# A float32 encoder trunk: two of the last projection's four column groups computed as seven products of half blocks

## The chip, the cores and the metric

The kernel runs on one core of a Trainium2 chip. Its engines are TensorE (PE; a weight load is PEld), VectorE (DVE), ScalarE (ACT), GpSimd (POOL) and SyncE (SP), which issues most of the transfers. They run side by side, each through its own list of instructions in order, and meet only in semaphores: an instruction waits until a counter has a value, and raises another when it is done. The metric is the device time of one launch in microseconds; lower is better.

## The reference

```python
for i in range(DEPTH):                       # DEPTH = 2: attention mixer, then conv mixer
    xn = _rmsnorm(x, norm_gain[i])
    y = _diff_attention(xn, ...) if i % 2 == 0 else _conformer_conv(xn, ...)
    x = x + y
return _rmsnorm(x, final_gain)

def _conformer_conv(xn, w_in, b_in, dw, dw_b, ln_g, ln_b, w_out, b_out):
    a, g, z = jnp.split(xn @ w_in + b_in, [CONV_WIDTH, 2 * CONV_WIDTH], axis=-1)
    u = a * jax.nn.sigmoid(g)
    u = depthwise_conv(u, dw) + dw_b         # 31 taps along the sequence
    u = silu(layernorm(u) * ln_g + ln_b)
    return (u * jax.nn.silu(z)) @ w_out + b_out
```

Shapes: x is 256 x 2048, every matrix float32. What changes is the last matrix product, `(u * silu(z)) @ w_out`, 256 x 2048 by 2048 x 2048, with the bias, the residual sum and the final norm around it.

## The kernel before, in words

**Products.** Each float32 product is made of three passes over operands that TensorE reads quickly: every operand is split into a high part (a rounded copy, by ScalarE, L476 for weights) and a low part (what is left, one subtraction of the operand and its high part: by VectorE at L826, by GpSimd at L448), and high x high, high x low and low x high are added up in PSUM.

**Weights.** They come in chunks of 128 x 4 x 512 (1 MB) through a ring of four raw buffers. SyncE loads chunk c when the low part of chunk c - 4 is made (`low_part_ready`, L317); ScalarE makes the high part, then VectorE or GpSimd the low part. `by_pool` (L298) says which: in most of the conv's input projection and the first four chunks of its output projection GpSimd, afterwards VectorE.

**Output projection of the conv.** Its 2048 columns are four groups of 512, each four chunks long (16 tiles of 128 along the contraction). For each tile there are two row tiles of x and three passes: 96 matmuls of 512 columns a group (`project`, L1237). The left operand is conv_hi and conv_lo. Before it lie the layer norm and the gating: VectorE normalises (L1118), ScalarE applies silu into PSUM banks (L673), VectorE multiplies with zT in place in PSUM (L1127, `gate_block`), ScalarE makes the high part (L681) and VectorE the low part (L1131, `block_lo`), eight blocks of two tiles each, which the first group waits for two by two. The counter s_lo counts them.

**Around it.** The bias and the final gain, each 128 x 2048, are loaded when s_lo is complete (L410, L412). VectorE adds the bias to the residual stream xs (L1163) and the product of each group to it (L1171), ScalarE sums squares (L785), VectorE multiplies by the gain (L1177). The last group is computed row tile by row tile on a bank that holds the bias and the residual already.

**Earlier stages that matter here.** After the attention's output projection VectorE turns x1 (L1017), makes its low parts (L1025), and works through low parts, the scaling of the first input group (L1070) and then 480 taps of the depthwise conv (L1065), in that order. Behind the taps come column sums, statistics, and a broadcast of them by TensorE (L1403), which TensorE reaches in its own order.

## Time and profile before

| | us |
|---|---|
| median of 3 runs (lowest, highest) | 827.04 (825.95, 827.09) |
| the profiled execution | 826.85 |
| its span, first to last instruction | 825.1 |
| TensorE busy | 817.6 |
| VectorE busy | 645.7 |
| ScalarE busy | 450.1 |
| GpSimd busy | 228.8 |

The mean granted clock of TensorE is 0.999 of full speed. "Busy" counts the time in which an instruction of the engine ran; in a timeline, "x4" at a row's end is the number of instructions merged into it, and what stands in brackets is the idle time before and what ended it.

### The profile page before, as it was taken

What the parts mean: (1) busy time and instruction counts of PE and PEld (TensorE: products, weight loads), DVE (VectorE), ACT (ScalarE), POOL (GpSimd) and SP (SyncE); (2) the same over time, 40 slices, a digit from 0 to 9 for tenths busy, and PEclk for the clock granted to TensorE, in tenths of its full rate; (3) what the DMA queues carried; (4) which work ended last, traced back from release to release, by engine and by line L of the source; (5) the groups of instructions that cost most, each with busy time, mean ns of one, the idle gap of its engine ahead of it and who ended that gap; (6) DMA issues with size and microseconds to landing.
All of it is one profiled execution on the core that took longest, in us unless ns stands there. A gap on an engine that the chain in (4) does not pass through costs nothing.

```text
span 825.1 us, 13852 instructions
## 1 busy us (share of the span) xinstructions
PE 817.6 (99%) x5628; PEld 756.1 (92%) x5628; DVE 645.7 (78%) x1099; ACT 450.1 (55%) x590; POOL 228.8 (28%) x107
## 2 busy tenths in 40 slices
PE   9999999999999999999999999999999999999996
PEld 9998899889998899888888999999999999998885
DVE  7578785697659785798788988999999998656651
ACT  7756643546436643556544465465555556694432
POOL 0300000000000000002000009988989887680000
PEclk9999999999999999999999999999999999999999
DMA  9987566536654566525655666655655565549502
GB/s 330 394 290 272 173 204 216 192 122 205 227 187 146 171 212 212 189 102 173 228 175 189 204 193 215 204 175 185 204 191 175 197 203 176 185 154 355 195 10 102
DMA packets 99809, 163.68 MB, mean 198 GB/s; under 512 B 3616, under 2 KB 40992, under 8 KB 99240
## 3 DMA queue, kind: packets, MB, share of 16 engines
q1 hardware_dynamic: 98128, 160.51, 57.8%
q10 hardware_dynamic: 1624, 2.38, 0.8%
q8 instruction: 39, 0.64, 0.3%
q14 instruction: 18, 0.15, 0.1%
HBM read 160.76 MB, written 3.69 MB: 199 GB/s over the span
## 4 chain that ended last, share of the span: by engine, by line
PE 56%; DVE 38%; ACT 4%; issue 2%; POOL 0%; ACTq 0%; DVEq 0%; POOLq 0%
DVE ps_d L1065 23%; PE ps_acc L1247 9%; PE ps_acc L1249 9%; PE ps_acc L1250 9%; PE ps_acc L1263 7%; PE ps_acc L1264 7%; PE ps_acc L1261 7%; DVE sb_w_lo L826 6%; DVE sb_zT L1017 3%; ACT sb_w_hi L476 2%; PE ps_acc L1307 1%; PE ps_acc L1311 1%; PE ps_acc L1314 1%; DVE sb_mT L980 1%; DVE sb_probs L948 1%
## 5 line engine op out<-in xcount | busy, mean ns | idle before, releaser
L476 ACT ACTIVATE sb_w_hi<-sb_w_raw 128x2048 fp32r<-128x2048 f32 x139 | 265.6, 1918 | 224.4 <-PE ps_acc L1264 151.9
L448 POOL TENSOR_TENSOR sb_w_lo<-sb_w_raw,sb_w_hi 128x2048 fp32r<-128x2048 f32 x45 | 208.2, 4633 | 389.2 <-ACT sb_w_hi L476 389.2
L826 DVE TENSOR_TENSOR sb_w_lo<-sb_w_raw,sb_w_hi 128x2048 fp32r<-128x2048 f32 x94 | 213.6, 2289 | 90.8 <-ACT sb_w_hi L476 90.4
L1261 PE MATMUL ps_acc<-sb_conv_hi,sb_w_hi 128*128 128x256 f32 x768 | 213.1, 278 | 0.0
L1264 PE MATMUL ps_acc<-sb_conv_hi,sb_w_lo 128*128 128x256 f32 x768 | 212.1, 276 | 0.0
L1263 PE MATMUL ps_acc<-sb_conv_lo,sb_w_hi 128*128 128x256 f32 x768 | 212.1, 276 | 0.0
L1065 DVE SCALAR_TENSOR_TENSOR ps_d<-sb_uT,sb_dwT,ps_d 128x256 f32<-128x256 f32 x480 | 189.0, 490 | 4.5 <-ACT ps_d L707 4.5
L1247 PE MATMUL ps_acc<-sb_w_hi,sb_act_hi 128*128 128x512 f32 x384 | 149.7, 390 | 0.0
L1249 PE MATMUL ps_acc<-sb_w_lo,sb_act_hi 128*128 128x512 f32 x384 | 149.6, 390 | 0.0
L1250 PE MATMUL ps_acc<-sb_w_hi,sb_act_lo 128*128 128x512 f32 x384 | 149.4, 389 | 0.0
L1263 PEld LDWEIGHTS ps_acc<-sb_conv_lo,sb_w_hi 128*128 128x128 f32 x768 | 144.2, 188 | 0.1
L1261 PEld LDWEIGHTS ps_acc<-sb_conv_hi,sb_w_hi 128*128 128x128 f32 x768 | 144.2, 188 | 0.1
L1264 PEld LDWEIGHTS ps_acc<-sb_conv_hi,sb_w_lo 128*128 128x128 f32 x768 | 144.2, 188 | 0.0
L1261 PE MATMUL ps_acc<-sb_act_hi,sb_w_hi 128*128 128x256 f32 x448 | 123.9, 276 | 0.0
L1264 PE MATMUL ps_acc<-sb_act_hi,sb_w_lo 128*128 128x256 f32 x448 | 123.7, 276 | 0.0
L1263 PE MATMUL ps_acc<-sb_act_lo,sb_w_hi 128*128 128x256 f32 x448 | 123.7, 276 | 0.0
L1250 PEld LDWEIGHTS ps_acc<-sb_w_hi,sb_act_lo 128*128 128x128 f32 x384 | 72.1, 188 | 15.1
L1247 PEld LDWEIGHTS ps_acc<-sb_w_hi,sb_act_hi 128*128 128x128 f32 x384 | 72.1, 188 | 15.0 <-DVE sb_act_lo L999 0.4
L1249 PEld LDWEIGHTS ps_acc<-sb_w_lo,sb_act_hi 128*128 128x128 f32 x384 | 72.1, 188 | 14.2
L1261 PEld LDWEIGHTS ps_acc<-sb_act_hi,sb_w_hi 128*128 128x128 f32 x448 | 84.1, 188 | 0.1
L1263 PEld LDWEIGHTS ps_acc<-sb_act_lo,sb_w_hi 128*128 128x128 f32 x448 | 84.1, 188 | 0.1
L1264 PEld LDWEIGHTS ps_acc<-sb_act_hi,sb_w_lo 128*128 128x128 f32 x448 | 84.1, 188 | 0.0
(171 smaller groups left out, 880.4 us busy)
## 6 DMA issues: line engine op xcount, KB each, us to landing
sb_w_raw<-in_attn_w_in SPq DMA_DIRECT2D x59, 1024.0 KB, 5.8
sb_w_raw<-in_conv_w_in SPq DMA_DIRECT2D x64, 512.0 KB, 4.6
sb_w_raw<-in_attn_w_out SPq DMA_DIRECT2D x16, 1024.0 KB, 5.0
sb_w_raw<-in_conv_w_in SPq DMA_DIRECT2D x16, 1024.0 KB, 5.1
sb_w_raw<-in_conv_w_out SPq DMA_DIRECT2D x16, 1024.0 KB, 5.0
sb_w_raw<-in_attn_w_in SPq DMA_DIRECT2D x15, 256.0 KB, 4.2
sb_xs<-in_x SPq DMA_DIRECT2D x2, 1024.0 KB, 12.3
sb_x_in<-in_x_turned SPq DMA_DIRECT2D x15, 128.0 KB, 4.0
```

The source lines that it names most:

```text
L448: pool.tensor_tensor(w_part(w_lo, c), w_raw[c % RING][:], w_part(w_hi, c).bitcast(F32), ALU.subtract).then_inc(lo_ready_pool, 1)
L476: act.activation(w_part(w_hi, c if like is None else like), w_raw[slot][:], ACT.Copy).then_inc(hi_ready, 1)
L826: dve.tensor_tensor(w_part(w_lo, like), w_raw[slot][:], w_part(w_hi, like).bitcast(F32), ALU.subtract).then_inc(lo_ready, 1)
L948: ins = dve.transpose(probs_turned[b * Q:(b + 1) * Q, :, :, a * Q:(a + 1) * Q], src[:, b])
L1017: ins = dve.transpose(dst, src)
L1065: dve.scalar_tensor_tensor(out_, uT[:, k, tap:tap + SEQ], dwT[:, k, tap:tap + 1], out_, ALU.mult, ALU.add).then_inc(tap_done, 1)
L1247: pe.matmul(into, left_hi, high[:, k], start=(kt == 0 and not filled), stop=False, skip_group_check=filled)
L1249: pe.matmul(into, left_hi, low[:, k], start=False, stop=False, skip_group_check=filled)
L1250: ins = pe.matmul(into, left_lo, high[:, k], start=False, stop=(kt == KT - 1), skip_group_check=filled)
L1261: pe.matmul(into, left_hi, hi[:, kt], start=(kt == 0 and f % 2 == 0), stop=False, skip_group_check=True)
L1263: pe.matmul(into, left_hi, lo[:, kt], start=False, stop=False, skip_group_check=True)
L1264: ins = pe.matmul(into, left_lo, hi[:, kt], start=False, stop=(kt == KT - 1), skip_group_check=True)
```

## The change

The second and third column group are computed together. In each of four quarters (two weight chunks: the same four tiles of the contraction, one for each group), the left operand is two row tiles by two halves of two tiles, the right one two halves by two column groups. Instead of eight half products there are seven, after Strassen's scheme in Winograd's form; B11, B21, T3, B22, T2, T4 and T1 name the right factors in the order of use. Each factor is 128 x 2 x 512: three are halves of the weights as loaded, and T3, T2, T4, T1 are sums, which GpSimd makes in place in the raw buffers. ScalarE makes each factor's high part and VectorE its low part. Each product is six matmuls of 512 columns, 42 a quarter. The seven products accumulate over the four quarters in seven banks, and VectorE adds these up at the end (`partial`). The left sums S1 to S4 are made once, by VectorE in zT, with high parts by ScalarE and low parts by VectorE.

For room and banks other things move. The gating writes zT instead of a PSUM bank, so block_hi and block_lo read zT. The bias is loaded early, behind the input projection's first four weight loads, and GpSimd adds it to all of xs in two operations of 128 x 2048. ScalarE copies xs into the banks that need it (`fill`). The gain is loaded into zT, behind the loads of the last quarter's chunks. The last group's banks are filled the same way, its first three low parts stay with VectorE and the last goes to GpSimd.

```diff
+SEVEN_AT = CHUNKS_CONV + NCH
+SEVEN_UPTO = SEVEN_AT + 2 * NCH
+QUARTERS = NCH
+B11, B21, T3, B22, T2, T4, T1 = range(7)
+FACTORS = (B11, B21, T3, B22, T2, T4, T1)
+S1, S2, S3, S4 = range(4)
...
+                b_out_bc = squared[:].rearrange("p a s n -> p (a s n)")
+                gain_bc = zT[:, 0:8].rearrange("p k s -> p (k s)")
...
-            return c == POOL_SEAM or POOL_FROM <= c < POOL_TO
+            return c == POOL_SEAM or POOL_FROM <= c < POOL_TO or c == CHUNKS - 1
...
+        def raw_factor(q, f):
+
+            c = SEVEN_AT + 2 * q + (f in (T3, B22, T1))
+            rows = HALVES[f in (B21, B22, T4)]
+            return w_raw[c % RING][:, rows]
+
+        def factor(parts, f):
+
+            at = ROWS_AT + f % 2 * 2 * GW
+            return parts[f // 2][:, at:at + 2 * GW].rearrange("p (k n) -> p k n", k=2)
+
...
+        SEVEN_BANKS = {B11: bank_a[1][:], B21: acc[:, 3], T3: bank_a[0][:], B22: acc[:, 2], T2: bank_d[0][:],
+                       T4: acc[:, 0], T1: bank_d[1][:]}
+        FILLED = (B21, B22, T4)
+        LAST_BANKS = (acc[:, 1], acc[:, 3])
+
+        def sums_in_place():
+
+            tiles = rows_and_tiles(zT)
+            (a11, a21), (a12, a22) = [[tiles[:, a, :, :, st * P:(st + 1) * P] for st in range(ST)] for a in range(2)]
+            return {S1: a22, S2: a11, S3: a21, S4: a12}
...
+                if g == 0:
+
+                    sp.wait_ge(ss_ready, ST + 2 * PAIRS)
+                    sp.dma_start(b_out_bc, bass.AP(conv_b_out.tensor, conv_b_out.offset, [[0, P], [1, D]])
+                                 ).then_inc(b_out_landed, 16)
+            while c < CHUNKS:
+                n, i = conv_out_chunk(c)
+                if of_seven(c - RING):
+                    sp.wait_ge(seven_lo, len(FACTORS) * ((c - RING - SEVEN_AT) // 2 + 1))
+                else:
                     low_part_ready(sp, c - RING)
-                    load(i, cw_out[:, i * CK:(i + 1) * CK, n * GW:(n + 1) * GW])
-                    c += 1
-                if n == 1:
-
-                    sp.wait_ge(s_lo, BLOCKS)
-                    sp.dma_start(b_out_bc[:], bass.AP(conv_b_out.tensor, conv_b_out.offset, [[0, P], [1, D]])
-                                 ).then_inc(final_landed, 16)
-                    sp.dma_start(gain_bc[:], bass.AP(final_gain.tensor, final_gain.offset, [[0, P], [1, D]])
+                load(c % RING, cw_out[:, i * CK:(i + 1) * CK, n * GW:(n + 1) * GW])
+                c += 1
+                if c == SEVEN_UPTO:
+
+                    sp.wait_ge(sum_lo, 4)
+                    sp.dma_start(gain_bc, bass.AP(final_gain.tensor, final_gain.offset, [[0, P], [1, D]])
                                  ).then_inc(final_landed, 16)
             for st in range(ST):
...
+
+            pool.wait_ge(b_out_landed, 16)
+            pool.wait_ge(x1_turned, PAIRS)
+            for st in range(ST):
+                pool.tensor_tensor(xs[:, st], xs[:, st], b_out_bc, ALU.add).then_inc(biased, 1)
...
+            for q in range(QUARTERS):
+                cx, cy = SEVEN_AT + 2 * q, SEVEN_AT + 2 * q + 1
+                b11, b21, b12, b22 = (raw_factor(q, f) for f in (B11, B21, T3, B22))
+                pool.wait_ge(landed[cy % RING], 16 * loads_of(cy))
+                pool.tensor_tensor(b12, b22, b12, ALU.subtract).then_inc(factor_ready, 1)
+                pool.wait_ge(landed[cx % RING], 16 * loads_of(cx))
+                pool.wait_ge(seven_lo, factors_done(q, B11))
+                pool.wait_ge(factor_ready, 4 * q + 1)
+                pool.tensor_tensor(b11, b12, b11, ALU.add).then_inc(factor_ready, 1)
+                pool.wait_ge(seven_lo, factors_done(q, B21))
+                pool.wait_ge(factor_ready, 4 * q + 2)
+                pool.tensor_tensor(b21, b21, b11, ALU.subtract).then_inc(factor_ready, 1)
+                pool.wait_ge(seven_lo, factors_done(q, T3))
+                pool.tensor_tensor(b12, b22, b11, ALU.subtract).then_inc(factor_ready, 1)
...
+                act.activation(block_of(conv_hi, b), block_of(zT, b), ACT.Copy).then_inc(s_hi, 1)
 
...
+            def factor_hi(q, f):
+
+                cx, cy = SEVEN_AT + 2 * q, SEVEN_AT + 2 * q + 1
+                if f in (B11, B21):
+                    act.wait_ge(landed[cx % RING], 16 * loads_of(cx))
+                elif f == B22:
+                    act.wait_ge(landed[cy % RING], 16 * loads_of(cy))
+                else:
+                    act.wait_ge(factor_ready, 4 * q + 1 + (T3, T2, T4, T1).index(f))
+                if q:
+                    act.wait_ge(seven_used, factors_done(q - 1, f))
+                else:
+                    act.wait_ge(w_free, SEVEN_AT + f // 2 + 1)
+                act.activation(factor(w_hi, f), raw_factor(q, f), ACT.Copy).then_inc(seven_hi, 1)
+
+            def fill(bank, n, st):
+
+                act.activation(bank, xs[:, st, n * GW:(n + 1) * GW], ACT.Copy).then_inc(bank_filled, 1)
+
+            def sum_high(i):
+
+                act.wait_ge(sum_ready, 4)
+                act.activation(sums_hi[:, i].rearrange("p (q k) s -> p q k s", k=2), sums_of_rows[i], ACT.Copy
+                               ).then_inc(sum_hi, 1)
+
+            sums_of_rows = sums_in_place()
+            factor_hi(0, B11)
+            factor_hi(0, B21)
+            act.wait_ge(acc_free, scaled_by(N_CONV - 1))
+            act.wait_ge(biased, ST)
+            fill(SEVEN_BANKS[B21], 1, 0)
+            fill(SEVEN_BANKS[B22], 2, 0)
+            for i in (S3, S4, S2, S1):
+                sum_high(i)
...
+            for f in (T3, B22, T2, T4):
+                factor_hi(0, f)
+            act.wait_ge(y_ready, 1)
+            fill(SEVEN_BANKS[T4], 1, 1)
+            factor_hi(0, T1)
+            act.wait_ge(sum_lo, 4)
+            for st in range(ST):
+                squares_of_y(0, st)
...
                 dve.wait_ge(z_done, 2 * (b + 1))
-                dve.tensor_tensor(gated_bank(b), gated_bank(b), block_of(zT, b), ALU.mult).then_inc(gated, 1)
...
+                dve.tensor_tensor(block_of(conv_lo, b), block_of(zT, b), block_of(conv_hi, b).bitcast(F32),
                                   ALU.subtract).then_inc(s_lo, 1)
...
+            def factor_lo(q, f):
+
+                dve.wait_ge(seven_hi, factors_done(q, f))
+                dve.tensor_tensor(factor(w_lo, f), raw_factor(q, f), factor(w_hi, f).bitcast(F32), ALU.subtract
+                                  ).then_inc(seven_lo, 1)
+
+            def row_sums():
+
+                s = sums_in_place()
+                a11, a12, a21, a22 = s[S2], s[S4], s[S3], s[S1]
+                dve.tensor_tensor(s[S1], a21, a22, ALU.add).then_inc(sum_ready, 1)
+                dve.wait_ge(sum_ready, 1)
+                dve.tensor_tensor(s[S3], a11, a21, ALU.subtract).then_inc(sum_ready, 1)
+                dve.wait_ge(sum_ready, 2)
+                dve.tensor_tensor(s[S2], s[S1], a11, ALU.subtract).then_inc(sum_ready, 1)
+                dve.wait_ge(sum_ready, 3)
+                dve.tensor_tensor(s[S4], a12, s[S2], ALU.subtract).then_inc(sum_ready, 1)
+
+            def sum_low(n, i):
+
+                dve.wait_ge(sum_hi, n + 1)
+                dve.tensor_tensor(sums_lo[:, i].rearrange("p (q k) s -> p q k s", k=2), sums_in_place()[i],
+                                  sums_hi[:, i].rearrange("p (q k) s -> p q k s", k=2).bitcast(F32), ALU.subtract
...
+            factor_lo(0, B11)
+            factor_lo(0, B21)
+            dve.wait_ge(s_lo, BLOCKS)
+            row_sums()
+            factor_lo(0, T3)
+            for n, i in enumerate((S3, S4, S2, S1)):
+                sum_low(n, i)
+            for f in (B22, T2, T4):
+                factor_lo(0, f)
+            dve.wait_ge(w_free, RING + CHUNKS_CONV + NCH)
+            for st in range(ST):
+                dve.tensor_tensor(y_of(0, st), acc[:, st], y_of(0, st), ALU.add).then_inc(y_ready, 1)
+            factor_lo(0, T1)
+            for f in FACTORS:
+                factor_lo(1, f)
+            dve.wait_ge(final_landed, 16)
             with_gain(0)
-            low_parts(6, 7)
-            with_product(1)
-            for st in range(ST):
-                dve.wait_ge(y_ready, 2 + st + 1)
-                with_bias(last, st, acc[:, 2 * (last % 2) + st])
-            low_parts(7, 10)
+            for q in range(2, QUARTERS):
+                for f in FACTORS:
+                    factor_lo(q, f)
+
...
+            def left_tiles(q, f, k):
+
+                if f in (B11, B21, T4):
+                    kt = CK * q + k + (0 if f == B11 else 2)
+                    rows = slice(P, 2 * P) if f == T4 else slice(0, P)
+                    return conv_hi[:, kt, rows], conv_lo[:, kt, rows]
+                i = {T3: S3, B22: S4, T2: S2, T1: S1}[f]
+                return sums_hi[:, i, 2 * q + k], sums_lo[:, i, 2 * q + k]
...
+            for q in range(QUARTERS):
+                for f in FACTORS:
+                    pe.wait_ge(seven_lo, factors_done(q, f))
+                    if q == 0:
+                        if f in FILLED:
+                            pe.wait_ge(bank_filled, FILLED.index(f) + 1)
+                        else:
+                            pe.wait_ge(gated, BLOCKS)
+                        if f in (T3, B22, T2, T1):
+                            pe.wait_ge(sum_lo, (T3, B22, T2, T1).index(f) + 1)
+                    into, high, low = SEVEN_BANKS[f], factor(w_hi, f), factor(w_lo, f)
+                    on = f in FILLED
+                    for k in range(2):
+                        left_hi, left_lo = left_tiles(q, f, k)
+                        end = q == QUARTERS - 1 and k == 1
+                        pe.matmul(into, left_hi, high[:, k], start=(q == 0 and k == 0 and not on), stop=False,
+                                  skip_group_check=on)
+                        pe.matmul(into, left_hi, low[:, k], start=False, stop=False, skip_group_check=on)
+                        ins = pe.matmul(into, left_lo, high[:, k], start=False, stop=end, skip_group_check=on)
+                    ins.then_inc(seven_used, 1)
+
+
             for st in range(ST):
```

VectorE, from the last two block subtractions on. Names: sb_w_lo is a low part of weights, seven_hi counts factors' high parts, sb_zT holds the left sums and, in its first half, the gain. The kernel before:

```order
L1131 TENSOR_TENSOR sb_conv_lo<-ps_d,sb_conv_hi 128x512 [waits s_hi]
L826 TENSOR_TENSOR sb_w_lo<-sb_w_raw,sb_w_hi 128x2048 [waits hi_ready] x4
L1163 TENSOR_TENSOR sb_xs<-sb_xs,sb_b_out_bc 128x512 [waits final_landed]
L1163 TENSOR_TENSOR sb_xs<-sb_xs,sb_b_out_bc 128x512
L1171 TENSOR_TENSOR sb_xs<-ps_acc,sb_xs 128x512 [waits y_ready_pre,w_free]
L1171 TENSOR_TENSOR sb_xs<-ps_acc,sb_xs 128x512 [waits y_ready_pre]
L1163 TENSOR_TENSOR sb_xs<-sb_xs,sb_b_out_bc 128x512 x4
L826 TENSOR_TENSOR sb_w_lo<-sb_w_raw,sb_w_hi 128x2048 [waits hi_ready] x2
L1177 TENSOR_TENSOR sb_xs<-sb_xs,sb_gain_bc 128x512 [waits ss_ready] x2
```

The same place of VectorE in the changed kernel, from the first factors on (its line numbers are its own):

```order
L1303 TENSOR_TENSOR sb_w_lo<-sb_w_raw,sb_w_hi 128x1024 [waits seven_hi] x2
L1310 TENSOR_TENSOR sb_zT<-sb_zT 128x4x2x128 [waits s_lo]
L1312 TENSOR_TENSOR sb_zT<-sb_zT 128x4x2x128 [waits sum_ready]
L1314 TENSOR_TENSOR sb_zT<-sb_zT 128x4x2x128 [waits sum_ready]
L1316 TENSOR_TENSOR sb_zT<-sb_zT 128x4x2x128 [waits sum_ready]
L1303 TENSOR_TENSOR sb_w_lo<-sb_w_raw,sb_w_hi 128x1024 [waits seven_hi]
L1321 TENSOR_TENSOR sb_sums_lo<-sb_zT,sb_sums_hi 128x1024 [waits sum_hi] x4
L1303 TENSOR_TENSOR sb_w_lo<-sb_w_raw,sb_w_hi 128x1024 [waits seven_hi] x3
L1353 TENSOR_TENSOR sb_xs<-ps_acc,sb_xs 128x512 [waits w_free]
L1353 TENSOR_TENSOR sb_xs<-ps_acc,sb_xs 128x512
L1303 TENSOR_TENSOR sb_w_lo<-sb_w_raw,sb_w_hi 128x1024 [waits seven_hi] x8
L1339 TENSOR_TENSOR sb_xs<-sb_xs,sb_zT 128x512 [waits ss_ready,final_landed]
```

Four low parts of 2048 elements are replaced by two of 1024, four row sums, one factor, four low parts of the sums, then factors again; the additions of the bias are gone; and the multiplication with the gain (L1339), with its wait on final_landed, stands behind 14 factors.

GpSimd, the end of its list. sb_w_raw is a raw weight chunk, factor_ready counts the sums and seven_lo the factors' low parts that VectorE made. Before:

```order
L448 TENSOR_TENSOR sb_w_lo<-sb_w_raw,sb_w_hi 128x2048 [waits hi_ready] x4
L461 TENSOR_TENSOR sb_uT<-sb_a_rows,sb_uT 128x256 [waits gate_ready] x2
L448 TENSOR_TENSOR sb_w_lo<-sb_w_raw,sb_w_hi 128x2048 [waits hi_ready] x4
L461 TENSOR_TENSOR sb_uT<-sb_a_rows,sb_uT 128x256 [waits gate_ready] x2
L448 TENSOR_TENSOR sb_w_lo<-sb_w_raw,sb_w_hi 128x2048 [waits hi_ready] x16
```

The end of GpSimd's list in the changed kernel, as far as the first quarter's sums:

```order
L524 TENSOR_TENSOR sb_uT<-sb_a_rows,sb_uT 128x256 [waits gate_ready] x2
L511 TENSOR_TENSOR sb_w_lo<-sb_w_raw,sb_w_hi 128x2048 [waits hi_ready] x16
L542 TENSOR_TENSOR sb_w_raw<-sb_w_raw 128x1024 [waits chunk_landed1]
L546 TENSOR_TENSOR sb_w_raw<-sb_w_raw 128x1024 [waits factor_ready,seven_lo,chunk_landed0]
L549 TENSOR_TENSOR sb_w_raw<-sb_w_raw 128x1024 [waits factor_ready,seven_lo]
L551 TENSOR_TENSOR sb_w_raw<-sb_w_raw 128x1024 [waits seven_lo]
```

Behind the low parts come sixteen sums, each waiting for low parts of VectorE (the rows repeat for each quarter), and one more low part at the end of the list.

SyncE, its last loads. Before:

```order
L345 DMA sb_w_raw<-in_conv_w_out 128x4x512 [waits lo_ready_pool] x8
L410 DMA sb_b_out_bc<-in_conv_b_out 128x2048 [waits s_lo]
L412 DMA sb_gain_bc<-in_final_gain 128x2048
L345 DMA sb_w_raw<-in_conv_w_out 128x4x512 [waits lo_ready] x8
L419 DMA out_x<-sb_xs 128x512 [waits out_ready]
```

SyncE's last loads in the changed kernel:

```order
L402 DMA sb_w_raw<-in_conv_w_out 128x4x512 [waits lo_ready_pool] x8
L402 DMA sb_w_raw<-in_conv_w_out 128x4x512 [waits seven_lo] x4
L475 DMA sb_zT<-in_final_gain 128x2048 [waits sum_lo]
L402 DMA sb_w_raw<-in_conv_w_out 128x4x512 [waits seven_lo] x4
L482 DMA out_x<-sb_xs 128x512 [waits out_ready]
```

The eight loads behind the factors wait on seven_lo, the bias's load has left this place, and the gain's stands behind the four loads for the third and the last quarter and ahead of those of the last group.

## Rows read from the trace of the kernel before

**Rows 1.** The page, parts 1 and 4: busy time and chain by engine
```profile
PE 817.6 (99%) x5628; PEld 756.1 (92%) x5628; DVE 645.7 (78%) x1099; ACT 450.1 (55%) x590; POOL 228.8 (28%) x107
...
PE 56%; DVE 38%; ACT 4%; issue 2%; POOL 0%; ACTq 0%; DVEq 0%; POOLq 0%
```

**Rows 2.** Busy time by stage; columns: stretch, length, then each engine, clock, DMA
```profile
753.40:797.00 43.60, 43.60 (x194) 36.10 (x193) 27.98 (x25) 17.81 (x16) 0.00 (x0) 1.00 0.49 169
...
819.00:822.50 3.50, 0.00 (x0) 0.00 (x0) 1.31 (x3) 2.05 (x5) 0.00 (x0) 1.00 0.34 125
822.50:825.10 2.60, 0.00 (x0) 0.00 (x0) 0.00 (x0) 0.00 (x0) 0.00 (x0) 0.57 0.63 235
```

**Rows 3.** Critical chain in order of time, 690 to 704 (start, us, what)
```profile
689.73 6.67 DVE ps_d L1065 x17
...
703.29 0.92 PE ps_d L1403 x3
```

**Rows 4.** Timeline of VectorE, 700 to 826 (start, us, engine, line, operation, idle)
```profile
739.69 0.69 DVE L1131 TENSOR_TENSOR sb_conv_lo<-ps_d,sb_conv_hi 128x512 fp32r<-128x512 f32 x1
...
775.22 1.29 DVE L1171 TENSOR_TENSOR sb_xs<-ps_acc,sb_xs 128x512 f32<-128x512 f32 x2 [1.14 <-PE ps_acc L1250]
...
796.98 1.29 DVE L1171 TENSOR_TENSOR sb_xs<-ps_acc,sb_xs 128x512 f32<-128x512 f32 x2 [1.14 <-PE ps_acc L1250]
```

**Rows 5.** Timeline of ScalarE, 700 to 826
```profile
741.49 1.28 ACT L481 ACT_TABLE_LOAD   x1
...
753.52 1.92 ACT L476 ACTIVATE sb_w_hi<-sb_w_raw 128x2048 fp32r<-128x2048 f32 x1 [3.52 <-PE ps_acc L1250]
...
818.74 0.60 ACT L798 ACTIVATE sb_junk<-ps_acc 128x512 f32<-128x512 f32 x1 [8.23 <-PE ps_acc L1250]
```

**Rows 6.** Lines by form (line, operation, forms, count, busy, mean ns, idle)
```profile
L461 POOL TENSOR_TENSOR sb_uT<-sb_a_rows,sb_uT 128x256 f32<-128x256 f32 x16 | 11.6, 747 | 28.0 <-ACT sb_a_rows L689 27.9
...
L868 DVE TENSOR_TENSOR sb_w_lo<-sb_w_raw,sb_w_hi 128x1024 fp32r<-128x1024 f32 x2 | 2.5, 1226 | 1.3 <-ACT sb_w_hi L507 1.3
L507 ACT ACTIVATE sb_w_hi<-sb_w_raw 128x1024 fp32r<-128x1024 f32 x2 | 2.1, 1063 | 1.1 <-DMA sb_w_raw<-in_attn_w_in 1.1
```

**Rows 7.** Timeline of VectorE, 445 to 500
```profile
478.82 1.67 DVE L1025 SCALAR_TENSOR_TENSOR sb_conv_lo<-sb_zT,sb_vec_all,sb_conv_hi 128x256 fp32r<-128x256 f32 x4
...
482.84 8.90 DVE L826 TENSOR_TENSOR sb_w_lo<-sb_w_raw,sb_w_hi 128x2048 fp32r<-128x2048 f32 x4 [1.12 <-ACT sb_w_hi L476]
...
497.47 2.84 DVE L1065 SCALAR_TENSOR_TENSOR ps_d<-sb_uT,sb_dwT,ps_d 128x256 f32<-128x256 f32 x7 [4.53 <-ACT ps_d L707]
```

**Rows 8.** Timeline of GpSimd, 700 to 826
```profile
723.01 18.41 POOL L448 TENSOR_TENSOR sb_w_lo<-sb_w_raw,sb_w_hi 128x2048 fp32r<-128x2048 f32 x4 [6.40 <-ACT sb_w_hi L476]
```

**Rows 9.** Line L440 alone (ns: min/median/max; first and last start)
```profile
L440 POOL COPY sb_line<-sb_table x31: 173/178/1202, 20.5 to 27.9; 8x1 f32<-8x1 f32 x15, 8x4 f32<-8x4 f32 x4, 8x165 f32<-8x165 f32 x2, 8x27 f32<-8x27 f32 x2
```

**Rows 10.** Timeline of all engines, 24.0 to 25.0
```profile
23.86 1.29 POOL L440 COPY sb_line<-sb_table 8x1 f32<-8x1 f32 x2
23.89 1.23 DVE L868 TENSOR_TENSOR sb_w_lo<-sb_w_raw,sb_w_hi 128x1024 fp32r<-128x1024 f32 x1 [1.25 <-ACT sb_w_hi L507]
```

**Rows 11.** Timeline of all engines, 384.5 to 388
```profile
384.37 4.03 DVE L980 STREAM_TRANSPOSE sb_mT<-sb_o_rows 32x256 f32<-32x256 f32 x9
384.46 4.62 POOL L448 TENSOR_TENSOR sb_w_lo<-sb_w_raw,sb_w_hi 128x2048 fp32r<-128x2048 f32 x1 [356.25 <-ACT sb_w_hi L476]
```

**Rows 12.** Timeline of ScalarE, 445 to 500
```profile
470.55 0.18 ACT L642 ACTIVATION_READ_ACCUMULATOR sb_squared<-sb_xs 128x1 f32 x1
```

**Rows 13.** DMA issues, 735 to 790 (KB each, median us to landing)
```profile
sb_w_raw<-in_conv_w_out SPq DMA_DIRECT2D x10, 1024.0 KB, 5.0
sb_b_out_bc<-in_conv_b_out SPq DMA_DIRECT2D x1, 1024.0 KB, 6.9
sb_gain_bc<-in_final_gain SPq DMA_DIRECT2D x1, 1024.0 KB, 8.9
```

150 lines of the change are left out of this document (85 added, 65 removed).

## Prediction, made before the changed kernel was run

> **What bounds the kernel now.** I read the page's busy shares first: TensorE is busy 99% of the span, but the chain that ended last runs 56% through PE and 38% through DVE [rows 1], so two engines share the bound. Then the busy time by stage: in the two column groups that change, 753.4 to 797, TensorE has no gap, at full clock, while VectorE is busy 28.0 of 43.6 us and GpSimd not at all [rows 2]. The critical chain in order of time shows where DVE's 38% lies: the taps run up to the layer norm, and TensorE's broadcast there (L1403) starts only when that chain arrives, at 703.29 [rows 3]. So there are two price lists: VectorE time lost before 703 goes straight into the end, and after 731 TensorE's own time does, as long as the others feed it.
>
> A column group of 96 products with 512 columns takes 21.76 us: the additions behind the second and third begin at 775.22 and 796.98 [rows 4]; that is 0.227 us a product, 1.36 us for six. ScalarE's first and last looks at accumulated rows put the end of the first group at 753.5 and TensorE's end at 818.7 [rows 5]; what follows that end stays.
>
> **The change part by part.** I work in the clock of the profiled execution (826.85 us, its span 825.1; the median 827.04 is 0.2 us above).
>
> *Removed:* 192 products become 168: 24 x 0.227 = 5.4 us of TensorE, all of it on the path. A quarter of the seven is 42 products, 9.5 us.
>
> *Added for VectorE, ScalarE and GpSimd, per quarter.* Seven low parts of 1024 elements on VectorE: 1.23 us alone [rows 6], 1.15 in a row (2048 elements take 2.2 each in a row of four [rows 7], and half of that and the constant part make 1.15). Seven high parts on ScalarE at 1.06 [rows 6], 0.97 in a row. Four in-place sums on GpSimd; the trace has no 1024 there, but 256 elements take 0.75 [rows 6] and 2048 take 4.60 (18.41 for four [rows 8]); on the line between them 2.4. Per quarter: VectorE 8.0, ScalarE 6.8, GpSimd 9.6, against TensorE's 9.5. If all four run side by side this is just level.
>
> *Do they run side by side?* That decides the case. GpSimd copies single columns of eight partitions at the start, again and again: the median is 0.178 us, the longest 1.202 [rows 9]. Two such copies last 1.29 us together while VectorE runs one subtraction of 1.23 that reads two SBUF tensors [rows 10]: the second copy began after it and ended with it, so it waited. Beside one-input transposes a 2048 subtraction of GpSimd runs at its usual 4.62 [rows 11]. The rest of GpSimd's subtractions before lie beside VectorE operations with an operand in PSUM, never beside one with two large SBUF inputs. The change brings exactly these together: 28 factor subtractions, four row sums and four low parts of these, eight block subtractions whose input moves from PSUM to zT, and the bias adds. The Trainium skill states the rule (SBUF — State Buffer, "Who interferes with whom"): a VectorE instruction with two SBUF inputs and a GpSimd instruction that reads SBUF share one read interface, and whichever issues second blocks until the other is done. By that rule the trace's copies had to wait, and VectorE has to wait in its turn, which no long row here shows.
>
> I take mutual exclusion, alternating where both want the interface: the simplest reading of rows 10, where the later one stood for the whole of the earlier. Ends: none at all (the lower sums below), and full 4.6 or 2.4 us waits for VectorE.
>
> *Bias adds moved to GpSimd (2 x 4.6).* They wait for the last turn of x1 and for a transfer that SyncE issues when the last square of x1 is summed, at 470.7 [rows 12], and that took 6.9 at its place before [rows 13]. So they are ready at 477.6, ahead of VectorE's L1025 at 478.82 [rows 7], which reads two SBUF tensors. Both adds get in, one ahead of its four parts and one between them: 9.2 us later. All up to the first tap at 497.47 hangs on it in VectorE's order [rows 7], and the taps on the first. Price +9.2, at the least 0.
>
> *Block subtractions.* GpSimd's low parts fill 723.0 to 741.4 [rows 8], where nearly all of the eight subtractions fall. The first waits until 727.6, the second until 732.8, the fifth 742.2, the sixth 747.4; the eighth comes at 753.0, not 739.7 [rows 4]. TensorE needs the eighth 2.7 us ahead of the group's end, at 750.8, so 10 us were in hand; the first column group ends at 758.6 instead of 753.5: +5.1 (0 without exclusion).
>
> *First quarter.* From the eighth: two low parts (to 756.3), GpSimd's T2 (758.7), a row sum, T4 (762.2), three dependent row sums at 1.26 (766.0), four high parts of the sums on ScalarE 3.9, its table load with what is behind it 1.5 [rows 5] and T3's high part 1.1 (772.4), then on the interface T3's low part, a sum's low part, T1, another, T3 of the next quarter, two more, and the low parts of B22, T2, T4: 8 x 1.15 + 2 x 2.4 (786.3). Two additions 1.2, fill and T1's high part 1.5 (which start inside), T1's low part, its product: 791.2. TensorE is there from 758.6: 32.6 us for 9.5. Without exclusion the same list gives 753.5 to 768.5, 15.0, since the sums' parts and B22 still stand in one queue on VectorE.
>
> *Quarters two to four.* The interface is held 7 x 1.15 + 4 x 2.4 = 17.6 us a quarter. ScalarE's squares and a fill put a gap of 1.4 ahead of the second, which takes 18.0. The third takes 18.1, the last 15.4 (no T3 behind it).
>
> *The gain's transfer.* with_gain(0) stands between VectorE's 14th and 15th factor and waits for a transfer that SyncE issues only after two weight loads, all three released by the 14th low part. A weight load lands 5.0 us after issue at the median; the gain before, issued right behind the bias, took 8.9 against its 6.9 [rows 13], so a transfer of 1 MB ahead costs 2.0 and the half us between the issues. Three deep I take 5.0 + 2 x 2.5 = 10. Nothing of the third quarter is prepared behind it on VectorE: TensorE's gap is 10.8 (bounds 8 and 12).
>
> *Last group.* Its low parts alternate with VectorE's additions of the partials: 1.1 us ahead of it and 24.7 for its 96 products instead of 21.7: +3.0 and +1.1.
>
> Sum after 731, with exclusion: 5.1 + 32.6 + 1.4 + 18.0 + 10.8 + 18.1 + 15.4 + 1.1 + 3.0 - 43.5 (the two groups before) = +62.0. With the bias adds +71.2, so 826.9 + 71.2 = 898. Two things are left out, of opposite sign: starting costs of an operation may hide behind the other engine's hold (0.15 us on each of some 25 changes, -4), and TensorE's clock: after it ends at 818.7 the granted clock is full until 822.5 and 0.57 on average in the rest [rows 2], so the idle stretches of 9 to 14 us here drop it to 1.2 GHz and the products behind them start at twice their time (+2 to +6). I take them as equal: 897.
>
> **The rivals.**
> 1. *Only GpSimd waits, VectorE never.* For it: only that side is seen in rows 9 and 10. The bias adds and the first group cost nothing, the first quarter 15.0, the other three stay at about 17.6, since GpSimd's 9.6 must fit beside VectorE's 8.0. That is 21 (next rival) + 3 x 6.7 = +41: 868.
> 2. *No exclusion between large operations.* First quarter 15.0, gap 1.4, then 11.0 each (B11's low part, three sums at 2.4, ScalarE and VectorE behind T1, as a chain), gap 11.0, last group +2.1 +2.2: +21, 848. Against it: rows 9 and 10.
> 3. *The other side: the factors stay ahead of TensorE.* Mechanism: VectorE, ScalarE and GpSimd at 8.0, 6.8 and 9.6 us a quarter, side by side, with the first quarter's factors ready by 753.5 and the gain landed before it is asked for. Then only the removed products count: 826.9 - 5.4 = 821.4. It decides at B22: if its low part is done by 757.5, TensorE never waits. It stands behind four row sums, four high parts and four low parts of these, which alone are 4 x 1.26 + 3.9 + 4.6 after 743; that is why I give it little.
> 4. *Worse than the sum:* a TensorE at 1.2 GHz over the whole stretch needs 42 x 0.43 = 18 us a quarter and becomes the longest: some 10 to 20 us more, 910 to 920.
>
> That fewer products are issued is sure: the order has 24 rows less on TensorE.
>
> **How the numbers follow.** Mutual exclusion 0.62 (own range 880 to 912), rival one 0.15, rival two 0.13, rival three 0.03, rival four 0.07. The predicted time is 897. The range 847 to 912 holds about 0.58 + 0.15 + 0.09. About 0.2% (1.7 us) is what this measurement tells from no change: faster 0.03, within 0.01, slower 0.96.
>
> **What would show it.** GpSimd's 1024 sums: 2.4 us alone, and 3.5 beside VectorE's; VectorE's 1024 subtractions at 1.23 in a row, and 2.4 us apart more where GpSimd works; the first tap at 506.7, not 497.5; TensorE's L1403 wait grown by some 9; conv_lo's eighth block about 13 us late; a TensorE gap of about 10 ahead of the fifteenth factor, released by the gain's transfer; quarters of 17.6 us. Quarters of 11 us would refute exclusion; a first tap in its old place would show that GpSimd alone waits.

## The result, and the profile after

The changed kernel takes 895.4 us (median of 6 runs, 895.3 to 896.4) against 827.1 (825.9 to 827.2): a ratio of 1.083, 95% interval 1.0819 to 1.0842. The forecast was 897. The profiled execution took 895.49 us with a span of 893.7, 68.6 us more than the one of before.

I read the page after first, parts 1, 2 and 4; in part 2 each digit is a fortieth of the span, and `PEclk` is the granted clock in tenths.

```profile
PE 826.7 (93%) x5604; PEld 755.9 (85%) x5604; DVE 725.0 (81%) x1122; ACT 470.0 (53%) x620; POOL 297.4 (33%) x126
...
PE   9999999999999999999996999999999999463776
...
POOL 1200000000000000020005398898888767244740
PEclk9999999999999999999998999999999999778899
...
PE 65%; DVE 21%; issue 4%; ACT 4%; DMA 3%; SPq 2%; POOL 1%; POOLq 1%; ACTq 0%; DVEq 0%
```

Two holes in TensorE's row answer to its 99% in [rows 1]: a small one in the 22nd slice, where 7.8 us of waiting for L1163 lie, and a deep one over the last six slices. Its busy time is up although 24 products are gone: a stretch at a lower clock takes longer for the same products (0.43 us each instead of 0.227, in rows further down). The waits of TensorE from 730 us say who keeps it (us in total, times, longest):

```profile
PE ps_a L1634 <- DVE sb_w_lo L1303: 13.9, 4, 10.8
PE ps_acc L1634 <- DVE sb_w_lo L1303: 13.5, 6, 5.9
PE ps_a L1634 <- DVE sb_sums_lo L1321: 12.7, 1, 12.7
PE ps_d L1634 <- DVE sb_w_lo L1303: 5.0, 3, 1.7
PE ps_acc L1426 <- DVE sb_conv_lo L1269: 2.1, 2, 1.9
PE ps_acc L1426 <- DVE sb_w_lo L1328: 2.0, 2, 1.2
PE ps_acc L1426 <- POOL sb_w_lo L511: 1.6, 1, 1.6
```

Before, TensorE had no gap in the two column groups [rows 2]. Now it waits 51 us in this stage, and all but 1.6 of them name VectorE.

Next the two places where the forecast saw VectorE and GpSimd meet. First the timeline of the bias stage (start, length, engine, line; in brackets the idle time ahead and its releaser), VectorE and then GpSimd; it answers to [rows 7]:

```profile
479.27 10.20 DVE L1163 SCALAR_TENSOR_TENSOR sb_conv_lo<-sb_zT,sb_vec_all,sb_conv_hi 128x256 fp32r<-128x256 f32 x4
...
499.57 2.29 DVE L964 TENSOR_TENSOR sb_w_lo<-sb_w_raw,sb_w_hi 128x2048 fp32r<-128x2048 f32 x1 [1.06 <-ACT sb_w_hi L560]
507.59 4.80 DVE L1203 SCALAR_TENSOR_TENSOR ps_d<-sb_uT,sb_dwT,ps_d 128x256 f32<-128x256 f32 x12 [4.53 <-ACT ps_d L789]
```

```profile
477.18 11.21 POOL L529 TENSOR_TENSOR sb_xs<-sb_xs,sb_squared 128x2048 f32<-128x2048 f32 x2 [10.69 <-DVE sb_zT L1155]
```

Four small VectorE instructions took 1.67 us before and take 10.20 beside the two bias adds; the first tap comes at 507.59 instead of 497.47.

Then the block subtractions, again VectorE first; they answer to [rows 4] and [rows 8]:

```profile
733.60 9.73 DVE L1269 TENSOR_TENSOR sb_conv_lo<-sb_zT,sb_conv_hi 128x512 fp32r<-128x512 f32 x2 [0.16 <-ACT sb_conv_hi L763]
...
747.94 9.69 DVE L1269 TENSOR_TENSOR sb_conv_lo<-sb_zT,sb_conv_hi 128x512 fp32r<-128x512 f32 x2 [1.07 <-ACT sb_conv_hi L763]
...
761.28 1.47 DVE L1269 TENSOR_TENSOR sb_conv_lo<-sb_zT,sb_conv_hi 128x512 fp32r<-128x512 f32 x2
```

```profile
733.13 9.65 POOL L511 TENSOR_TENSOR sb_w_lo<-sb_w_raw,sb_w_hi 128x2048 fp32r<-128x2048 f32 x2 [6.40 <-ACT sb_w_hi L560]
```

Without GpSimd at work two of them take 1.47 us (the last row), with it 9.7. Note that no gap of that size stands ahead of the long ones: the wait is inside the duration, so a view of waits by semaphore does not show it. So the engines do not meet only in semaphores, as the section on the chip had it: VectorE and GpSimd also meet here. The second quarter of the seven products, and what follows it, VectorE and GpSimd:

```profile
799.42 16.80 DVE L1303 TENSOR_TENSOR sb_w_lo<-sb_w_raw,sb_w_hi 128x1024 fp32r<-128x1024 f32 x7 [1.48 <-ACT sb_w_hi L873]
826.50 1.29 DVE L1339 TENSOR_TENSOR sb_xs<-sb_xs,sb_zT 128x512 f32<-128x512 f32 x2 [10.27 <-DMA sb_zT<-in_final_gain]
```

```profile
804.18 3.17 POOL L549 TENSOR_TENSOR sb_w_raw<-sb_w_raw 128x1024 f32<-128x1024 f32 x1
807.31 3.37 POOL L551 TENSOR_TENSOR sb_w_raw<-sb_w_raw 128x1024 f32<-128x1024 f32 x1
```

Seven low parts that need 8.0 us in a row take 16.8, and each GpSimd sum 3.2 to 3.4. Behind them VectorE stands for the gain's transfer.

### The profile page after: what moved, and what is told of

It reads as the page before. It is cut to its first block, busy times and chain, and to the rows that moved or that the text cites. A ratio compares the mean times of both kernels' runs of the same rounds, so it can differ in the third digit from the quotient of the medians.

```text
span 893.7 us, 13912 instructions
## 1 busy us (share of the span) xinstructions
PE 826.7 (93%) x5604; PEld 755.9 (85%) x5604; DVE 725.0 (81%) x1122; ACT 470.0 (53%) x620; POOL 297.4 (33%) x126
## 4 chain that ended last, share of the span: by engine, by line
PE 65%; DVE 21%; issue 4%; ACT 4%; DMA 3%; SPq 2%; POOL 1%; POOLq 1%; ACTq 0%; DVEq 0%
PE ps_acc L1440 14%; PE ps_acc L1443 14%; PE ps_acc L1442 14%; PE ps_acc L1426 6%; PE ps_acc L1428 6%; PE ps_acc L1429 6%; DVE sb_w_lo L964 4%; DVE sb_w_lo L1303 4%; DVE sb_zT L1155 3%; DMA sb_xs<-in_x 2%; DVE sb_conv_lo L1163 2%; ACT sb_w_hi L560 1%; DVE sb_conv_lo L1269 1%; DMA sb_zT<-in_final_gain 1%; DVE sb_sums_lo L1321 1%
## 5 line engine op out<-in xcount | busy, mean ns | idle before, releaser
L511 POOL TENSOR_TENSOR sb_w_lo<-sb_w_raw,sb_w_hi 128x2048 fp32r<-128x2048 f32 x46 | 213.4, 4643 | 407.0 <-ACT sb_w_hi L560 393.9
L560 ACT ACTIVATE sb_w_hi<-sb_w_raw 128x2048 fp32r<-128x2048 f32 x127 | 242.5, 1917 | 195.9 <-PE ps_acc L1443 152.3
L964 DVE TENSOR_TENSOR sb_w_lo<-sb_w_raw,sb_w_hi 128x2048 fp32r<-128x2048 f32 x82 | 186.2, 2288 | 71.9 <-ACT sb_w_hi L560 71.5
```

Source lines behind the costliest of these rows:

```text
L511: pool.tensor_tensor(w_part(w_lo, c), w_raw[c % RING][:], w_part(w_hi, c).bitcast(F32), ALU.subtract).then_inc(lo_ready_pool, 1)
L560: act.activation(w_part(w_hi, c if like is None else like), w_raw[slot][:], ACT.Copy).then_inc(hi_ready, 1)
L964: dve.tensor_tensor(w_part(w_lo, like), w_raw[slot][:], w_part(w_hi, like).bitcast(F32), ALU.subtract).then_inc(lo_ready, 1)
```

## The experiments

Theory: a VectorE instruction with two SBUF inputs and a GpSimd instruction that reads SBUF take turns, each waiting for the whole of the other; the gain's place costs 10 us more. The rivals are that only GpSimd waits, that there is no exclusion and the sums' own length or ScalarE's chain sets the quarters, and that the bias stage's delay has another cause. Times are medians of 4 runs, of ports_alone of one; the kernel before took 827.0 to 827.6 beside them.

**The two engines by themselves** (ports_alone). The kernel holds nothing but ten stages, each a number of VectorE's instructions and a number of GpSimd's, with separate operands for each engine:

```diff
+ def v_two(dve, i):
+     return dve.tensor_tensor(vout[i][:], va[:], vb[:], ALU.subtract)
...
+ def p_two_1024(pool, i):
+     return pool.tensor_tensor(pout[i][:, 0:N], pa[:, 0:N], pb[:, 0:N], ALU.subtract)
...
+ STAGES = (
+     (v_two, 8, None, 0),
+     (None, 0, p_two_1024, 4),
+     (None, 0, p_two_2048, 2),
+     (v_two, 10, p_two_1024, 4),
+     (v_two, 8, p_two_2048, 3),
+     (v_psum, 10, p_two_1024, 4),
+     (v_copy, 10, p_two_1024, 4),
+     (v_scalar, 10, p_two_1024, 4),
+     (v_two, 8, p_copy, 4),
+     (v_two, 8, p_memset, 4),
+ )
```

> No kernel of the task: ten stages one after the other, each a run of 8 or 10 VectorE instructions of 128 x 1024 and 2 to 4 GpSimd instructions with nothing that orders them inside a stage (x is copied to the output). Theory (alternation of whole instructions; either engine waits where VectorE reads two SBUF tensors and GpSimd reads SBUF): alone, VectorE's subtraction takes 1.22 (1.14 in a row), GpSimd's 2.2 to 2.4 for 1024 and 4.6 for 2048. Together: while both have work, GpSimd's 1024 show 3.3 and VectorE's turn comes once per GpSimd instruction, 3.3 us apart; beside GpSimd's 2048 VectorE's come 5.7 us apart; both stages last as long as the two lists one after the other (10 x 1.14 + 4 x 2.2 = 20). VectorE with one operand in PSUM: no waits, both as alone, 11.5 in all. VectorE with one SBUF input (copy, multiply by a number): no waits either, or, if these take the same path in a faster mode, waits as with two. GpSimd's memset, which reads nothing: no waits; its copy: waits. Rival A (shared bandwidth, not turns): both engines' instructions are longer by one steady factor, and VectorE's take some 2 us each instead of a mix of 1.2 and 3.3. Rival B (only GpSimd waits): VectorE's stay at 1.14 throughout and GpSimd's first takes the 9 us that VectorE's list takes.

Timeline of its stages, first each engine alone:

```profile
8.44 9.17 DVE L96 TENSOR_TENSOR sb_vout<-sb_va,sb_vb 128x1024 f32<-128x1024 f32 x8
17.76 9.23 POOL L108 TENSOR_TENSOR sb_pout<-sb_pa,sb_pb 128x1024 f32<-128x1024 f32 x4 [17.32 <-DVE sb_vout L96]
27.14 8.95 POOL L111 TENSOR_TENSOR sb_pout<-sb_pa,sb_pb 128x2048 f32<-128x2048 f32 x2
```

Then the first turns of the stage with both, from narrow windows on it; GpSimd's four, and its three of 2048:

```profile
36.22 1.22 DVE L96 TENSOR_TENSOR sb_vout<-sb_va,sb_vb 128x1024 f32<-128x1024 f32 x1 [18.61 <-POOL sb_pout L111]
37.36 3.36 DVE L96 TENSOR_TENSOR sb_vout<-sb_va,sb_vb 128x1024 f32<-128x1024 f32 x1
39.60 3.32 POOL L108 TENSOR_TENSOR sb_pout<-sb_pa,sb_pb 128x1024 f32<-128x1024 f32 x1
...
36.23 13.25 POOL L108 TENSOR_TENSOR sb_pout<-sb_pa,sb_pb 128x1024 f32<-128x1024 f32 x4
56.32 16.40 POOL L111 TENSOR_TENSOR sb_pout<-sb_pa,sb_pb 128x2048 f32<-128x2048 f32 x3 [6.84 <-DVE sb_vout L96]
```

And the stages in which one of the two reads otherwise:

```profile
78.37 11.41 DVE L99 TENSOR_TENSOR sb_vout<-ps_bank,sb_vb 128x1024 f32<-128x1024 f32 x10
78.42 9.28 POOL L108 TENSOR_TENSOR sb_pout<-sb_pa,sb_pb 128x1024 f32<-128x1024 f32 x4 [5.70 <-DVE sb_vout L96]
89.81 14.69 DVE L102 COPY sb_vout<-sb_va 128x1024 f32<-128x1024 f32 x10
89.86 11.08 POOL L108 TENSOR_TENSOR sb_pout<-sb_pa,sb_pb 128x1024 f32<-128x1024 f32 x4 [2.17 <-DVE sb_vout L99]
119.28 11.44 POOL L114 COPY sb_pout<-sb_pa 128x2048 f32<-128x2048 f32 x4 [3.62 <-DVE sb_vout L105]
135.26 7.04 POOL L117 MEMSET sb_pout<- 128x2048 f32 x4 [4.54 <-DVE sb_vout L96]
```

The first subtraction runs undisturbed (1.22), the next takes 3.36 because GpSimd's stands in between, and GpSimd's takes 3.32 instead of 2.31 because it waited for VectorE's. Some are undisturbed and some wait for a whole instruction, so bandwidth is not shared evenly (rival A falls), and VectorE waits as much as GpSimd (rival B falls). Beside GpSimd's three of 2048, each of these takes 5.5 instead of 4.5. VectorE's subtractions alone start every 1.135 us ((9.17 - 1.22) / 7). Both lists together last 56.3 - 36.2 = 20.1 us; one after the other they would last 10 x 1.135 + 9.2 = 20.6, so each of GpSimd's turns hides some 0.13 us. With one operand in PSUM the two run as if alone (11.41 and 9.28). VectorE's copy of a single SBUF tensor does not escape: GpSimd's four grow from 9.2 to 11.1, and of the ten copies half take 0.69 or less, the longest 2.83. GpSimd's copy, with one SBUF input, holds VectorE up too: eight subtractions last 16.0 beside four of them, not 9.2 (how long the copy takes alone was not run). Its memset (7.04 for four) leaves VectorE at 9.2 for eight, as alone.

**The bias adds behind the first gates** (bias_later).

```diff
+                if c == POOL_FROM:
+                    pool.wait_ge(b_out_landed, 16)
+                    pool.wait_ge(x1_turned, PAIRS)
+                    for st in range(ST):
+                        pool.tensor_tensor(xs[:, st], xs[:, st], b_out_bc, ALU.add).then_inc(biased, 1)
                 low_part(c)
```

> Only the place of GpSimd's two bias adds differs from the changed kernel: behind the gates of the first tap pair instead of beside VectorE's x1_low parts. Theory (a VectorE instruction with two SBUF inputs and a GpSimd instruction that reads SBUF alternate): the four x1_low parts go back from 10.2 to about 1.7 us, the first tap from 507.6 to about 497.5, the two adds take 4.6 us each beside the taps and cost the taps nothing, and GpSimd's low parts have some 9 us in hand there; time 895.4 - 10.1 = 885.3. Rival A (the 10 us come from something else that the change did at this place, the transfer of the bias or the ring of loads): the tap stays at 507 and the time at 895. Rival B (GpSimd's low parts have no 9 us in hand): the tap is early but TensorE waits for GpSimd's first low parts of the conv stage, 885 plus up to 9.

891.4 us: only 4.0 back. VectorE's rows of the stage, then GpSimd's:

```profile
479.00 1.67 DVE L1163 SCALAR_TENSOR_TENSOR sb_conv_lo<-sb_zT,sb_vec_all,sb_conv_hi 128x256 fp32r<-128x256 f32 x4
498.83 12.63 DVE L1203 SCALAR_TENSOR_TENSOR ps_d<-sb_uT,sb_dwT,ps_d 128x256 f32<-128x256 f32 x32 [4.53 <-ACT ps_d L789]
...
526.90 8.33 DVE L1203 SCALAR_TENSOR_TENSOR ps_d<-sb_uT,sb_dwT,ps_d 128x256 f32<-128x256 f32 x21 [3.27 <-ACT ps_d L789]
```

```profile
496.82 9.25 POOL L535 TENSOR_TENSOR sb_xs<-sb_xs,sb_squared 128x2048 f32<-128x2048 f32 x2
...
524.33 1.45 POOL L524 TENSOR_TENSOR sb_uT<-sb_a_rows,sb_uT 128x256 f32<-128x256 f32 x2
```

The cause is confirmed: x1_low is back at 1.67 and the first tap comes 8.8 us earlier than in the changed kernel. But GpSimd's next gates come late (524.33), and the taps of that pair wait 3.3 for them, by way of ScalarE's L789; 1.4 of the tap's delay stay with the early transfer. Rival B was nearly right, with another victim: the taps, not TensorE, which waits 1.5 once for GpSimd. The last 1.4 us stand in the trace at the layer norm. There the broadcast L1582 starts 2.6 us behind VectorE's last statistic (706.81 to 709.40); in the changed kernel it is 1.2 (712.21 to 713.39). TensorE has waited 2.4 for ScalarE's L801 behind the taps, and of its products between that wait and the broadcast, those from 703.2 to 706.8 take 0.21 us each instead of 0.12. That the slow products are the reason for the 1.4 is read from these rows; no run tests it.

**One bias add in each of two later groups** (bias_spread), with the bias's transfer two groups later too.

```diff
+                if f == 0 and n in (Z_FROM - 1, Z_FROM):
+                    st = n - Z_FROM + 1
+                    ...
+                    pool.tensor_tensor(xs[:, st], xs[:, st], b_out_bc, ALU.add).then_inc(biased, 1)
```

> Place of the two bias adds again: one ahead of GpSimd's first low part in each of two neighbouring column groups without gates (z groups), the transfer two groups later. Theory: the first tap is back at 497.5 without the 1.1 and 0.6 us waits for high parts that the early transfer brought, GpSimd has 21.8 - 18.4 = 3.3 us a group to spare there and some 7 in hand, so neither TensorE nor the taps wait: 895.4 - 10.1 = 885.3. Rival (GpSimd has nothing in hand in that stage either; the place behind the first gates gave back 6 of 10): 888 to 892.

885.6 us, ratio to before 1.0711 (1.0693 to 1.0729). The tap is back in its place, and TensorE has no wait in the whole conv stage:

```profile
497.30 2.45 DVE L1204 SCALAR_TENSOR_TENSOR ps_d<-sb_uT,sb_dwT,ps_d 128x256 f32<-128x256 f32 x6 [4.53 <-ACT ps_d L790]
```

So the bias step, adds and transfer, cost 9.8 us, all of it by its place.

**The gain's transfer ahead of two weight loads** (gain_earlier).

```diff
-                if c == SEVEN_UPTO:
+                if c == SEVEN_UPTO - 2:
```

> Only SyncE's order differs: the gain's transfer is issued ahead of the two weight loads of the fourth quarter instead of behind them. Theory (the 10.3 us wait is nothing but the place of the issue behind the 14th low part): the transfer is issued near 797, has landed by 812, VectorE's wait for it at 816 is gone, TensorE's gap of 10.8 ahead of the 15th factor falls to the 1.7 of the other factors, and the clock does not fall there either; time 895.4 - 10.3 = 885.1, down to 884 by the clock. Rival (what stands behind the wait would have been late anyway: high parts or loads of the third quarter): 890 to 895.

885.5 us, 9.9 less. The wait is gone between these two rows of VectorE, and the quarters stay as long as they were:

```profile
799.18 16.80 DVE L1303 TENSOR_TENSOR sb_w_lo<-sb_w_raw,sb_w_hi 128x1024 fp32r<-128x1024 f32 x7 [1.47 <-ACT sb_w_hi L873]
815.90 1.28 DVE L1339 TENSOR_TENSOR sb_xs<-sb_xs,sb_zT 128x512 f32<-128x512 f32 x2
817.11 31.28 DVE L1303 TENSOR_TENSOR sb_w_lo<-sb_w_raw,sb_w_hi 128x1024 fp32r<-128x1024 f32 x14
```

**The sums of weight blocks on VectorE, and left out** (sums_by_vector, no_sums). The first, cut:

```diff
+            for f, then in ((B11, T3), (B21, T2), (T3, T4), (B22, T1), (T2, None), (T4, None), (T1, None)):
+                factor_lo(q, f)
+                if then is not None:
+                    factor_sum(q, then)      # the sum that GpSimd made, by VectorE
```

The second drops the loop over the quarters on GpSimd and ScalarE's waits for `factor_ready`; raw blocks stand in for the sums, so its output is another one.

> GpSimd's sixteen sums of weight blocks are made by VectorE, set between its low parts; nothing else differs from the changed kernel. Theory (one read path, alternation): a quarter takes 11 x 1.15 = 12.7 us of VectorE instead of 16.7 with GpSimd in turns, so three quarters give 3 x 4.0 = 12, and the first some 4: 879 (875 to 884), although VectorE gets 16 x 1.15 = 18.4 us more work. Rival (VectorE never waits for GpSimd, its own queue and the additions are what the stage waits for): the 18.4 us come on top, 913.

> The sixteen sums of weight blocks are left out altogether (raw blocks take their place, so the output is another one); products, high parts and low parts stay. Theory: VectorE needs 7 x 1.15 = 8.1 us a quarter and TensorE 9.5 at full clock, so TensorE is the longer again and quarters two to four take 9.6 each: 3 x 7.1 = 21 less, the first quarter 8 less; 866 (862 to 870). Rival (the quarter's length is VectorE's low parts with their waits for ScalarE, not the sums): quarters stay near 16.7 and the time at 890 or more.

882.4 and 864.1 us: 13.1 and 31.3 less. VectorE has 18.4 us more work in the first and the kernel is faster for it. The rows of VectorE, first in sums_by_vector: the third quarter's first low part, the sum behind it, and the instruction that follows the fourth quarter. Then, in no_sums, the low parts of the third and fourth quarter:

```profile
819.74 1.22 DVE L1289 TENSOR_TENSOR sb_w_lo<-sb_w_raw,sb_w_hi 128x1024 fp32r<-128x1024 f32 x1
820.88 1.22 DVE L1333 TENSOR_TENSOR sb_w_raw<-sb_w_raw 128x1024 f32<-128x1024 f32 x1
...
844.72 0.68 DVE L1381 TENSOR_TENSOR sb_xs<-sb_zT,ps_acc 128x512 f32<-128x512 f32 x1
```

```profile
810.37 15.98 DVE L1287 TENSOR_TENSOR sb_w_lo<-sb_w_raw,sb_w_hi 128x1024 fp32r<-128x1024 f32 x14
```

Two quarters take 844.72 - 819.74 = 25.0 us in the first, 12.5 each, as expected; with GpSimd in turns they took 31.3 with one sum fewer in them, and without sums VectorE needs 8.0 a quarter. That the sums' own length or ScalarE's chain sets the quarter is refuted.

**The blocks' product in PSUM again** (blocks_from_psum). The gate writes PSUM and block_hi reads it there too (not shown below); the row sums read zT without the gate, so the output is another one.

```diff
-                dve.tensor_tensor(block_of(conv_lo, b), block_of(zT, b), block_of(conv_hi, b).bitcast(F32),
+                dve.tensor_tensor(block_of(conv_lo, b), gated_bank(b), block_of(conv_hi, b).bitcast(F32),
```

> The gate's product stays in its PSUM bank, and ScalarE's high part and VectorE's low part of each block read it there, as in the kernel before; everything else is as in the changed kernel (the row sums then read zT without the gate, so the output is another one). Theory (VectorE with one operand in PSUM does not share GpSimd's read path): the eighth block's low part comes at 739.7 + 10.1 = 749.8 instead of 762.7, TensorE's first column group ends without its waits of 1.9 and 0.2, VectorE's list of the first quarter starts 12.9 earlier; the end comes 12.9 earlier too, 882.5, or somewhat less (8) where the first quarter then waits for slots that TensorE frees at the end of its group. Rival (GpSimd's low parts cost the blocks only what the move to zT costs by itself): the blocks' times stay, 894 to 896.

886.5 us, 8.9 less. The last block's low part starts at 749.36, and behind it:

```profile
749.36 0.69 DVE L1269 TENSOR_TENSOR sb_conv_lo<-ps_d,sb_conv_hi 128x512 fp32r<-128x512 f32 x1
750.31 5.24 DVE L1303 TENSOR_TENSOR sb_w_lo<-sb_w_raw,sb_w_hi 128x1024 fp32r<-128x1024 f32 x2 [0.26 <-ACT sb_w_hi L873]
```

12.7 us earlier, as expected; then 2.9 are given back at once, since the first two factors now meet the end of GpSimd's low parts (5.24 instead of 2.36).

**Fewer products in the kernel before** (fewer_products): in `project`, the product `left_hi x low` is skipped three times in each of the eight chunks.

> The kernel before with 24 products left out of its second and third column groups (high x low, three in each of the eight chunks), and nothing else, so the output is another one: what the scheme takes off TensorE, by itself. Theory (TensorE is the bound from 731 on): 24 x 0.227 = 5.4 us, 821.6. Rival (the low parts and high parts of the chunks are only just in time, so TensorE waits for them as soon as it is faster): 823 to 827.

821.8 us, ratio 0.9941 (0.9924 to 0.9957): 5.2 less. This is what the scheme takes off TensorE, and it was sized rightly.

**The seven products with all this mended** (seven_best): bias_spread, the gain's issue early, sums_by_vector, the gate's product in PSUM with ScalarE copying it to zT, and the row sums in two halves.

```diff
+            def row_sums(half):
+                s = {i: t[:, 2 * half:2 * half + 2] for i, t in sums_in_place().items()}
+                ...
             block_lo(5)
+            row_sums(0)
```

> The seven products with what the other runs showed: bias adds spread over two z groups, gain's transfer issued early, factor sums on VectorE, gate's product in PSUM (ScalarE copies it to zT), row sums of the first and second half apart, the first half ahead of the last two blocks. Theory (VectorE is now the stage's bound: 11 x 1.14 = 12.55 us a quarter against TensorE's 9.5): from 743 VectorE has 4 x 12.55, two halves of low parts of the row sums 5.2, the second half's sums 2.5 and four additions 2.6, which is 804; then 3.5 to the first low part of the last group, 21.8 of products and 8 behind them: 838 (834 to 845), still slower than before. Rival A (ScalarE's chain of high parts, 7 x 1.0 a quarter and the row sums' own, sets the quarters): 845 to 855. Rival B (VectorE gets so far ahead during the first column group that TensorE never waits): 821.

851.2 us, ratio 1.0291 (1.0274 to 1.0308): 44 of the 68 us are undone, but 13 fewer than I expected. VectorE's list begins at 750.7 instead of 743, and 5.3 us of that are the theory's own mechanism, overlooked by me: the first half's row sums stand where GpSimd still makes low parts (one from 738.70 to 743.37).

```profile
736.48 1.70 DVE L1272 TENSOR_TENSOR sb_zT<-sb_zT 128x512 f32<-128x512 f32 x1
738.21 0.69 DVE L1274 TENSOR_TENSOR sb_zT<-sb_zT 128x512 f32<-128x512 f32 x1
738.94 4.98 DVE L1276 TENSOR_TENSOR sb_zT<-sb_zT 128x512 f32<-128x512 f32 x1
```

One of 0.69 took 1.70, another 4.98. The other 2.4 I put down to ScalarE's added copies ahead of the blocks, without a run for it; what the traces show is that VectorE's waits for the blocks' high parts come to 6.4 us here and to 3.4 in blocks_from_psum, which has no such copies. 2.6 more are three waits of VectorE for ScalarE (1.0, 0.9 and 0.7), and the last group takes some 3 us more than its products: TensorE waits 1.6 there for GpSimd's low part, and for VectorE's. The quarters are as expected, from the third's first low part at 788.87 to the last at 813.9, 12.5 each.

**The same with the sums left out** (best_no_sums): `factor_sum` returns at once.

> The kernel of seven_best with the sixteen sums of weight blocks left out (raw blocks in their place, so the output is another one): what the scheme would be worth if its sums cost nothing. Theory (the shared read path and VectorE's time are the whole loss): in seven_best TensorE's first column group ended at 755.5; four quarters of 9.5 us behind it without a wait, 2 us for the first low parts that stand behind the row sums, then 21.8 for the last group: TensorE ends at 819.3, and with the 8.1 us that lie between TensorE's end and the time of the kernel before the time is 827.4 (825 to 831): a tie with the kernel before, because the first column group still ends late. Rival A (something else holds the quarters at 12.5, ScalarE's high parts or the additions): 840 to 851. Rival B (without the sums the removed products show in full): 821.

835.6 us, ratio 1.0105 (1.0088 to 1.0122), 8 above what I expected. Rival A, quarters of 12.5 us, is refuted: VectorE's last two take 16.0 together, and in the first two TensorE waits 0.5 and 1.3 us. It then waits 4.4 for the third quarter's first factor, ahead of which VectorE has the row sums' low parts and the gain, and three waits for ScalarE (2.6, 0.9 and 0.7), whose list holds the second half's row sums and a table load there:

```profile
783.37 0.79 PE L1645 MATMUL ps_a<-sb_w_hi,sb_conv_hi 128*128 128x512 f32 x1 [4.39 <-DVE sb_w_lo L1320]
```

So even with free sums this arrangement does not reach 827. Whether another one could with the sums in it was not tried; VectorE's 12.5 us a quarter against the 10.9 that two column groups cost TensorE before (43.5 / 4) speak against it.

## Why the prediction was right

The mechanism that decided it, alternation, was read from one instruction of 1.29 us in [rows 10] and the maximum in [rows 9]; the runs bear it out for every size. The terms:

| step | predicted | measured in the trace after |
|---|---|---|
| bias adds, to the first tap | +9.2 | +10.1 |
| first column group | +5.1 | +4.4 (ends 768.1; 753.5 + 10.1 before) |
| first quarter | 32.6 | 32.0 (to 800.1) |
| gap and second quarter | 1.4 + 18.0 | 0.6 + 17.5 |
| gain's transfer | 10.8 | 10.8 |
| third and fourth quarter | 18.1 + 15.4 | 17.3 + 14.9 |
| gap and last group | 1.1 + 24.7 | 0.8 + 25.4 |
| less the two groups before and 21.7 | -65.2 | -65.2 |
| sum | +71.2 | +68.6 |

1. *Bias stage.* The order was as forecast, one add ahead of x1_low and one inside. The 10.1 are 8.5 inside x1_low (10.20 - 1.67), 0.45 of a later start, and 1.06 of a wait for a high part, which the forecast lacked: the bias transfer stands ahead of the weight loads. With the transfer two groups later that wait is gone (bias_spread), and bias_later kept 1.4.
2. *Blocks.* The eighth came 12.7 late by the run that undid it alone; the forecast said 13.3. But the eighth is not what TensorE waits for. It waits 1.9 us for the sixth and, at 762.11, 0.2 for the seventh; the 24 products from there end the group at 768.1. By the forecast's own words (13.3 late, 10 in hand) the price was 3.3; its 5.1 does not follow from them, and that it lies near the measured 4.4 is luck.
3. *Quarters.* The forecast took 17.6; VectorE's rows give 31.3 for the last two and 16.8 for the second. Two things make the difference, both seen in ports_alone: a sum of GpSimd takes 2.31 and not 2.4, and a start of 0.13 hides behind the other engine's turn. 7 x 1.135 + 4 x (2.31 - 0.13) is 16.7. The forecast had named that overlap and left it out.
4. *Clock.* Products behind a long idle stretch come at 0.43 us each instead of 0.227:

```profile
792.26 0.80 PE L1634 MATMUL ps_acc<-sb_w_hi,sb_sums_hi 128*128 128x512 f32 x1 [5.88 <-DVE sb_w_lo L1303]
792.85 0.63 PE L1636 MATMUL ps_acc<-sb_w_lo,sb_sums_hi 128*128 128x512 f32 x1
793.27 0.63 PE L1637 MATMUL ps_acc<-sb_w_hi,sb_sums_lo 128*128 128x512 f32 x1
```

That is the 1.2 GHz level: from 829 to 834 us, where they run without a gap, the granted clock is 0.50. It cost next to nothing: these products end at 800.06, and the next factor's low part keeps TensorE waiting for 0.64 more; behind the gain's gap the slow products end 0.9 ahead of the next factor. The forecast's +2 to +6 for the clock was the term that was sized wrongly, and it had been set against an overlap of -4; of the two, only the overlap came, so the sum is 2.6 under +71.2. The total, only 1.6 us off, is somewhat better than its terms: their misses, from -1.3 to +0.9 a row, cancel in part, and with clock and overlap taken as equal the sum stays 898, so that the 897 holds 1 us that nothing explains.
5. *One sign failed.* The forecast expected TensorE's wait at the broadcast (L1403, now L1582) to grow by 9. TensorE has no wait there; it waits 7.8 us for L1163's parts at the bias stage instead and comes to the broadcast late already. The price was the same: the broadcast came 10.1 us later (713.39 instead of 703.29).

The Trainium skill (SBUF — State Buffer, "Who interferes with whom") says that the interface is held for a whole instruction, that order of issue decides who blocks, and that a VectorE copy in its two-port mode takes it too. ports_alone agrees with the first two: 3.36 beside 1.22, with the engine that came second waiting, in turn. Its copies cost GpSimd 1.9 us over four sums, which agrees with the third, though no run shows in which mode they ran. The section's exception for instructions of GpSimd that only write agrees with VectorE's 9.2 beside the memsets.

Of the rivals: the first (only GpSimd waits) is refuted by L1163 and by VectorE's row of 3.36; the second and third by the quarters; the fourth (a slow TensorE throughout) by the granted clock, 0.7 to 0.9 over the stage instead of 0.5, in part 2 of the page.

## What to carry to other kernels

Before work is given to an idle GpSimd, or an operand is moved from PSUM to SBUF, list what VectorE does at the same time: beside its instructions with two SBUF inputs (or a copy of one) GpSimd's stand in line and hold the way for twice as long, so that VectorE making the sum itself is sooner (12.5 us a quarter instead of 16.7). The wait stands inside both engines' durations, so compare the mean length of the same instruction with and without company, not the waits. A scheme that trades TensorE's products for elementwise sums is to be priced by the engines that make its operands: here 5.2 us of products against 31 for the sums of weight blocks on GpSimd.

## What the runs showed of the hardware that was not expected

- A VectorE copy of 128 x 1024 f32 with one SBUF input, and a multiplication by a number, also take turns with GpSimd's two-input subtraction: ten of them last 14.7 us beside four of GpSimd's, which take 11.1 instead of 9.2; the longest copy takes 2.83, most of them 0.69. Before, only one-input transposes had been seen beside GpSimd, and those do not wait [rows 11].

Two more facts had been expected and are now measured. A GpSimd copy of 2048 elements (one SBUF input) makes VectorE's two-input subtractions wait: eight last 16 us beside four copies instead of 9.2. GpSimd beside taps with one operand in PSUM does not wait: the two bias adds took 9.25 there, as two of [rows 8] do.
